# Stick-breaking attention with queries on partitions: reversed scans on VectorE for matrix sums on TensorE, and a gate product on GpSimd

## The chip, the cores and the metric

The kernel runs on one core of one Trainium2 chip. The number is the device time of one execution in microseconds (us), the median over repeated runs. Engines are named as in the profile: PE (TensorE matmul, with PEld for its weight loads), DVE (VectorE), ACT (ScalarE), POOL (GpSimd), SP (the queue that issues the weight transfers).

## What is computed

Two transformer blocks on 512 tokens of width 1024. The first has pooling, a gated unit, cross attention and a feed-forward part; the second has stick-breaking attention beside a gated 31-tap convolution, and a feed-forward part. The change is in the second block:

```python
def stick_breaking_attention(q, k, v):      # 8 heads of 64
    # A[t,s] = beta[t,s] * prod_{s<j<t} (1 - beta[t,j]),  beta = sigmoid(q_t.k_s / 8), s < t
    ...
        z = jnp.einsum("bqhd,bkhd->bhqk", qb, kb) * scale
        mask = s_idx < t_idx
        log_beta = jax.nn.log_sigmoid(z)
        log_one_minus = jnp.where(mask, jax.nn.log_sigmoid(-z), 0.0)
        tail = lax.cumsum(log_one_minus, axis=3, reverse=True) - log_one_minus
        weights = jnp.where(mask, jnp.exp(log_beta + tail), 0.0)
        outs.append(jnp.einsum("bhqk,bkhd->bqhd", weights, vb))
...
        c = glu_a * jax.nn.sigmoid(glu_b)
        c = causal_depthwise_conv(c, conv_dw_w[layer], conv_dw_b[layer])   # 31 taps
        c = jax.nn.silu(layer_norm(c, conv_ln_g[layer], conv_ln_b[layer]))
        mixed = jnp.concatenate([attn, c], axis=-1) @ w_out[layer]
```

## The kernel before

Every large product is made to nearly full fp32 precision from two rounded parts: three matmuls for each 128 x 128 piece of a weight (high x high, high x low, low x high, lines 1258 to 1260). The weights come as 216 blocks of 128 x 1024 through a ring of four slots. SP loads a block, ACT rounds it (`w_hi`, 1.05 us), POOL makes the rest (`w_lo`, two halves, L365), PE takes 24 matmuls of 512 columns with it. Each engine runs an order written out by hand, and semaphores join them.

The second block begins with the gated unit: 8 blocks `GLU` (gate and value in turns), then 4 blocks for the values `v2`, then 8 blocks for queries and keys (`qk_block(t)`, q and k of one pair of heads in turns). During `GLU` DVE multiplies the gate by the root of the norm (L1133), ACT takes the sigmoid (L646), DVE multiplies the value bank by the root (L1137) and then by the sigmoid (L1141). DVE fills the rest of its time with the 120 taps of the convolution (`conv_taps`, L1126); the first 68 stand before the q and k work, the other 52 are dealt out between its steps.

The attention goes by pairs of heads, each head's 1280 score columns in three PSUM banks, so two heads fill six banks. Keys are on the partitions and queries along the columns, in four tiles (512, 384, 256 and 128 columns, `TILES`). For a pair:

- `pair_scores(j)` on PE: eight matmuls, and six that add -1e30 where the key isn't before the query.
- `s_logs(hd)` on ACT: three activations over 1280 columns (a cap at 40, exp, and log of one plus that).
- `s_softplus(hd)` on DVE: the maximum with the scores (L1159), then three small adds into `later_sums` (L1165, L1168).
- `s_cumulate(hd)` on PE: nine fp32 matmuls with a matrix of -1 in a triangle (`neg_tri`) and one full of -1 (`neg_ones`), which add minus the sum over later keys to the scores in PSUM (L1582).
- `s_weights(hd)` on ACT: exp of that in two parts (L702). The next pair's scores take the same banks, so they wait for it (`s_att`).
- `pair_values(j)` on PE: weights times `v2`; ACT and DVE split the result in two parts (`pair_values_hi`, `pair_values_lo`).

Between them stand each q or k block's own steps: `qk_input` (DVE, frees the bank), `qk_squares_of` (ACT, which also rounds the next weight block), `qk_sum` (PE), `qk_rstd_of` (ACT, log and exp), `qk_apply` (DVE). After the last pair comes the layer norm of the convolution: POOL adds the four channel tiles (L443, wait for the last tap), PE sums over partitions (`ln_channel_sums(0)`), DVE subtracts the mean (`ln_centre`), ACT squares, POOL adds, PE sums again (`ln_channel_sums(1)`), ACT makes the root and, with another function table (L756), the silu. The output product `output2(m, ks)` can take the parts k = 0 to 3 (attention) early and needs k = 4 to 7 (convolution) at the end.

## Time and profile before

| | us |
|---|---|
| median of 3 runs | 1230.31 (1230.0 to 1230.79) |
| the profiled execution | 1230.45 |
| its span in the trace | 1228.7 |
| PE busy | 1222.5 (99%) |
| DVE busy | 593.9 (48%) |
| POOL busy | 585.3 (48%) |
| ACT busy | 505.4 (41%) |

The span is what the trace covers; 1.75 us of the execution lie around it. The granted TensorE clock is full in every slice. The stage of the change runs from 661 us (the gated unit) to about 843 us (the end of the first four output blocks' work). A busy PE is not PE at its peak: the record of a 512-column matmul is 0.39 us long, but one starts every 0.227 us.

### The profile page before, as it was taken

The numbers are of one execution on the slowest core, as the hardware profiler recorded it, in microseconds if no ns is written. First come the engines' busy times: TensorE is split into PE (matmuls) and PEld (weight loads), VectorE is DVE, ScalarE is ACT, GpSimd is POOL, SyncE is SP. The second block draws the span as 40 slices with busy tenths as digits, with TensorE's granted clock in tenths as the row PEclk, the third lists the DMA queues.
The fourth block names the chain that finished last, engine by engine and source line by source line (L and its number), as shares of the span: only waits on it lengthen the run. The fifth ranks groups of instructions, "written<-read, shape, count | busy, mean of one in ns | idle before, by whom it ended". The sixth has DMA issues, their size and how long they took to land.

```text
span 1228.7 us, 16447 instructions
## 1 busy us (share of the span) xinstructions
PE 1222.5 (99%) x5590; PEld 1004.1 (82%) x5590; DVE 593.9 (48%) x870; ACT 505.4 (41%) x677; POOL 585.3 (48%) x473
## 2 busy tenths in 40 slices
PE   9999999999999999999999999999999999999998
PEld 7988888888888888888888886768888888888887
DVE  6782435434653165414675898764333223321431
ACT  7532443343443144323464247675433223332331
POOL 5875553233445344463465652134444434444444
PEclk9999999999999999999999999999999999999999
DMA  7444332122232322232233221102222322223222
GB/s 299 138 138 135 105 103 69 52 69 69 103 102 103 103 85 87 101 120 72 77 125 103 103 86 52 35 18 86 87 102 88 117 86 102 93 83 116 81 77 82
DMA packets 34035, 118.41 MB, mean 96 GB/s; under 512 B 4033, under 2 KB 4161, under 8 KB 33857
## 3 DMA queue, kind: packets, MB, share of 16 engines
q1 hardware_dynamic: 33696, 117.49, 27.9%
q8 instruction: 34, 0.56, 0.2%
q10 hardware_dynamic: 288, 0.24, 0.1%
q14 instruction: 17, 0.13, 0.0%
HBM read 115.61 MB, written 2.10 MB: 96 GB/s over the span
## 4 chain that ended last, share of the span: by engine, by line
PE 93%; DVE 5%; ACT 1%; POOL 0%; issue 0%; POOLq 0%
PE ps L1258 29%; PE ps L1259 29%; PE ps L1260 29%; DVE ps L1126 2%; DVE slab L1126 2%; PE ps L1582 2%; PE ps L1425 1%; PE ps L1563 1%; PE ps L1324 0%; PE ps L1350 0%; PE ps L1623 0%; POOL squares L443 0%; PE ps L1440 0%; PE ps L1399 0%; PE ps L1536 0%
## 5 line engine op out<-in xcount | busy, mean ns | idle before, releaser
L365 POOL TENSOR_TENSOR w_lo<-w_raw,w_hi 128x512 fp32r<-128x512 f32 x430 | 557.3, 1320 | 610.3 <-ACT w_hi L476 355.8
L1258 PE MATMUL ps<-xg_hi,w_hi 128*128 128x512 f32 x960 | 375.8, 391 | 0.0
L1260 PE MATMUL ps<-xg_hi,w_lo 128*128 128x512 f32 x960 | 373.6, 389 | 0.0
L1259 PE MATMUL ps<-xg_lo,w_hi 128*128 128x512 f32 x960 | 373.6, 389 | 0.0
L1258 PE MATMUL ps<-y_hi,w_hi 128*128 128x512 f32 (+1 forms) x608 | 230.9, 380 | 0.0
L1259 PE MATMUL ps<-y_lo,w_hi 128*128 128x512 f32 (+1 forms) x608 | 229.8, 378 | 0.0
L1260 PE MATMUL ps<-y_hi,w_lo 128*128 128x512 f32 (+1 forms) x608 | 229.8, 378 | 0.0
L1260 PEld LDWEIGHTS ps<-xg_hi,w_lo 128*128 128x128 f32 x960 | 180.2, 188 | 37.7
L1258 PEld LDWEIGHTS ps<-xg_hi,w_hi 128*128 128x128 f32 x960 | 180.2, 188 | 37.7 <-issue 0.8
L1259 PEld LDWEIGHTS ps<-xg_lo,w_hi 128*128 128x128 f32 x960 | 180.2, 188 | 37.3 <-issue 0.5
L476 ACT ACTIVATE w_hi<-w_raw 128x1024 fp32r<-128x1024 f32 x124 | 130.4, 1051 | 126.1 <-PE ps L1260 126.1
L774 DVE TENSOR_TENSOR ps<-ps,rstd_bc 128x512 f32<-128x512 f32 x92 | 64.0, 698 | 184.7 <-PE ps L1260 182.6
L464 ACT ACTIVATE w_hi<-w_raw 128x1024 fp32r<-128x1024 f32 x91 | 96.0, 1055 | 96.2 <-PE ps L1260 79.9
L1259 PEld LDWEIGHTS ps<-y_lo,w_hi 128*128 128x128 f32 x608 | 114.4, 188 | 21.8 <-issue 0.5
L1258 PEld LDWEIGHTS ps<-y_hi,w_hi 128*128 128x128 f32 x608 | 114.4, 188 | 21.8 <-issue 0.6
L1260 PEld LDWEIGHTS ps<-y_hi,w_lo 128*128 128x128 f32 x608 | 114.4, 188 | 21.3
L517 ACT ACTIVATE slab<-ps,cols 128x512 f32<-128x512 f32 x66 | 51.3, 779 | 129.9 <-DVE ps L774 129.9
L892 DVE TENSOR_TENSOR h<-ps,h 128x512 f32<-128x512 f32 x32 | 22.1, 692 | 129.2 <-PE ps L1260 129.2
L523 ACT ACTIVATE slab<-slab 128x512 f32<-128x512 f32 x44 | 27.8, 632 | 120.2 <-DVE slab L872 120.2
L805 DVE TENSOR_TENSOR y_lo<-slab,y_hi 128x512 f32 (+1 forms) x52 | 37.9, 734 | 40.6 <-ACT y_hi L525 38.3
L525 ACT ACTIVATE y_hi<-slab 128x512 f32 x44 | 27.8, 632 | 66.1 <-DVE slab L878 44.9
L866 DVE SCALAR_TENSOR_TENSOR slab<-ps,cols,slab 128x511 f32<-128x511 f32 x66 | 49.0, 744 | 10.6 <-ACT slab L517 10.6
(218 smaller groups left out, 1064.1 us busy)
## 6 DMA issues: line engine op xcount, KB each, us to landing
w_raw<-weights SPq DMA_DIRECT2D x199, 512.0 KB, 3.2
w_raw<-weights SPq DMA_DIRECT2D x16, 384.0 KB, 2.9
out_t<-h SPq DMA_DIRECT2D x8, 256.0 KB, 2.0
h<-x_t SPq DMA_DIRECT2D x3, 512.0 KB, 8.3
slab<-mem_t SPq DMA_DIRECT2D x2, 512.0 KB, 10.6
slab<-mats_in SPq DMA_DIRECT2D x1, 1024.0 KB, 5.5
w_raw<-weights SPq DMA_DIRECT2D x2, 256.0 KB, 3.5
h<-x_t SPq DMA_DIRECT2D x2, 256.0 KB, 4.3
```

The lines of the kernel that those rows point to most:

```text
L365: nc.gpsimd.tensor_tensor(w_lo[:, s, half], w_raw[:, s, half], w_hi[:, s, half].bitcast(F32), ALU.subtract).then_inc(done, 1)
L464: nc.scalar.activation(w_hi[:, s, :], w_raw[:, s, :], ACT.Copy).then_inc(w_hi_ready, 1)
L476: nc.scalar.activation(w_hi[:, s, :], w_raw[:, s, :], ACT.Copy).then_inc(w_hi_ready, 1)
L517: nc.scalar.activation(acc[:, s + v, :], ps[:, s + v, :], ACT.Identity, scale=col(w, pair + (2 * n_w + v * FT)), bias=col(b, pair + v * FT ...
L523: nc.scalar.activation(acc[:, s, :], acc[:, s, :], ACT.Silu).then_inc(f_silu, 1)
L774: return nc.vector.tensor_tensor(out, ps[:, bank, 0:width], by[:, 0:width], ALU.mult)
L805: nc.vector.tensor_tensor(dst, src, hi.bitcast(F32), ALU.subtract).then_inc(y_lo_ready, 1)
L866: nc.vector.scalar_tensor_tensor(out=acc[:, s + v, 1:], in0=ps[:, s + v, 0:SEQ - 1], scalar=col(w, pair + (n_w + v * FT)), in1=acc[:, s + ...
L1126: nc.vector.scalar_tensor_tensor(out=conv_acc(i)[:, j:], in0=conv_in[:, i, 0:SEQ - j], scalar=col("conv_dw_w_2", (TAPS - 1 - j) * 4 + i), ...
L1258: pe.matmul(out, w[0], x[0], start=first, stop=False)
L1259: pe.matmul(out, w[0], x[1], start=False, stop=False)
L1260: return pe.matmul(out, w[1], x[0], start=False, stop=last)
```

## The change

**Layout.** The scores are made with queries on the partitions and keys along the columns: `pair_scores` takes q as the stationary and k as the moving operand. The tiles keep their sizes.

**Attention weights.** For each head ACT makes two sigmoids of the scores, beta into `took` and 1 - beta into the old stick tile, each over 1280 columns. DVE runs four `tensor_tensor_scan` over them with a reversed access pattern, state = (1 - beta) x state + beta, in place in `took` (`s_scan`, 512, 384, 256 and 128 columns). The result at key s is the sum of the weights of keys s and later. PE turns it with ten 128 x 128 transposes per head (`s_turn`) into the score banks, and ACT copies it out in one piece (`s_weights`, Copy over 1280 columns). The sum over later keys is not differenced again: the values are. `v2` becomes v[s] - v[s-1]: ACT issues two transfers that shift `v2` by a row, and POOL makes four subtractions (`v2_steps`).

**Function tables.** Sigmoid is not in the table set of log and exp, so ACT loads a table before each pair's sigmoids and another behind them: eight more table loads.

**Order.** `s_cumulate`, `s_logs`, `s_softplus` and `later_sums` are gone. `qk_block(5)` now stands ahead of `pair_values(0)`, `qk_block(6)` behind `pair_scores(2)`, and `s_turn(5)` behind `qk_block(7)`. `ln_channel_sums(0)` stood ahead of `output2(0, (2,))`; now it stands behind `pair_values(3)` and six output parts (m = 1 and 2, k = 0 to 2), and `ln_channel_sums(1)` behind four more. DVE leaves 4 taps behind the last scan.

**Gated unit.** POOL multiplies the sigmoid by the root (`glu_gate`), and DVE's product L1137 goes.

```diff
             for b in range(GLU, V2 + 4):
                 weights_lo_next(b)
+                if b < V2 and (b - GLU) % 2 == 0:
+                    i = (b - GLU) // 2
+                    pool.wait_ge(glu_sig, i + 1)
+                    nc.gpsimd.tensor_tensor(k2[:, i, :], k2[:, i, :], rstd_bc[:], ALU.mult).then_inc(glu_gate, 1)
...
-            for b in range(QK, WOUT2):
+            weights_lo_next(QK)
+            pool.wait_ge(v2_shifted, 32)
+            for t in range(ST):
+                nc.gpsimd.tensor_tensor(v2[:, t, :], v2[:, t, :], v2_before[:, t, :], ALU.subtract).then_inc(v2_steps, 1)
+                if t % 2:
+                    weights_lo_next(QK + 1 + t // 2)
+            for b in range(QK + 3, WOUT2):
                 if b == QK + 4:
-                    pool.wait_ge(s_later, 2)
+                    pool.wait_ge(s_summed, 2 * ST)
...
+            act.dma_start(v2_before[1:P, :, :], v2[0:P - 1, :, :]).then_inc(v2_shifted, 16)
+            act.dma_start(v2_before[0:1, 1:ST, :], v2[P - 1:P, 0:ST - 1, :]).then_inc(v2_shifted, 16)
...
+                nc.scalar.activation(took_of(hd), z_of(hd), ACT.Sigmoid).then_inc(s_parts, 1)
+                nc.scalar.activation(stick_of(hd), z_of(hd), ACT.Sigmoid, scale=-1.0).then_inc(s_parts, 1)
...
             def s_weights(hd):
-                for part, c in enumerate((FIRST, REST)):
-                    act.wait_ge(s_cum, 2 * hd + (2 if hd == SPLIT_HEAD else part + 1))
-                    nc.scalar.activation(stick_of(hd)[:, c], z_of(hd)[:, c], ACT.Exp).then_inc(s_att, 1)
+                act.wait_ge(s_turned, hd + 1)
+                nc.scalar.activation(stick_of(hd), z_of(hd), ACT.Copy).then_inc(s_att, 1)
...
+            def s_scan(hd):
+
+                dve.wait_ge(s_parts, 2 * hd + 2)
+                for bank, at, n in TILES:
+                    c = slice(bank * SEQ + at, bank * SEQ + at + n)
+                    took = backwards(took_of(hd)[:, c])
+                    nc.vector.tensor_tensor_scan(took, backwards(stick_of(hd)[:, c]), took, 0.0, ALU.mult,
+                                                 ALU.add).then_inc(s_summed, 1)
...
+            def s_turn(hd):
+
+                for n, t in enumerate((3, 2, 1, 0)):
+                    bank, at, _ = TILES[ST - 1 - t]
+                    pe.wait_ge(s_summed, ST * hd + n + 1)
+                    for key in range(t + 1):
+                        src = bank * SEQ + at + key * P
+                        to = AT[key] + (t - key) * P
+                        mm = pe.transpose(z_of(hd)[:, to:to + P], took_of(hd)[:, src:src + P], ident[:])
+                mm.then_inc(s_turned, 1)
```

PE, from the fourth root's sum to the second pair's scores: before, the sums over later keys of head 0 (the rows of head 1 read the same) and the start of pair 1.

```order
L1536 MATMUL ps<-squares,pair_ones 128x512 [waits qk_square]
L1582 MATMUL ps<-slab,neg_tri 128x512 [waits s_stick]
L1582 MATMUL ps<-slab,neg_ones 128x128
L1582 MATMUL ps<-later_sums,neg_ones 128x256 [waits s_later]
L1582 MATMUL ps<-slab,neg_tri 128x384
L1582 MATMUL ps<-slab,neg_tri 128x256
L1582 MATMUL ps<-slab,neg_tri 128x128
L1582 MATMUL ps<-slab,neg_ones 128x128 x2
L1582 MATMUL ps<-later_sums,neg_ones 128x128 [waits s_later]
```

The same place with the change: each tile's transposes wait for that tile's scan.

```order
L1539 MATMUL ps<-squares,pair_ones 128x512 [waits qk_square]
L1585 MATMUL ps<-ident,took 128x128 [waits s_summed]
L1585 MATMUL ps<-ident,took 128x128 x3
L1585 MATMUL ps<-ident,took 128x128 [waits s_summed]
L1585 MATMUL ps<-ident,took 128x128 x2
L1585 MATMUL ps<-ident,took 128x128 [waits s_summed]
L1585 MATMUL ps<-ident,took 128x128
L1585 MATMUL ps<-ident,took 128x128 [waits s_summed] x2
```

Nine matrix products that waited for `s_stick` and `s_later` have become ten transposes that wait for four scans; the last row's second instruction opens head 1.

ACT, around the scores of the last pair (heads 6 and 7): before, the root of the last k block, the split head 6 and head 7.

```order
L702 ACTIVATE slab<-ps 128x768 [waits s_cum]
L672 ACTIVATE slab<-ps,z_max 128x768 [waits s_out,s_z]
L674 ACTIVATE slab<-slab,z_max 128x768 [waits s_min]
L676 ACTIVATE slab<-slab 128x768 [waits s_exp]
L672 ACTIVATE slab<-ps,z_max 128x512
L674 ACTIVATE slab<-slab,z_max 128x512 [waits s_min]
L676 ACTIVATE slab<-slab 128x512 [waits s_exp]
L706 ACTIVATE y_hi<-ps 128x512 [waits s_out]
L670 ACTIVATE squares<-squares 128x1280 [waits s_last_min,s_out,s_z]
L676 ACTIVATE squares<-squares 128x1280 [waits s_exp]
```

The same place with the change.

```order
L694 ACTIVATE ps<-ps 128x512 [waits qk_log]
L685 ACT_TABLE_LOAD
L681 ACTIVATE took<-ps 128x1280 [waits s_out,s_turned,s_z]
L682 ACTIVATE slab<-ps 128x1280
L681 ACTIVATE took<-ps 128x1280 [waits s_out,s_turned,s_z]
L682 ACTIVATE squares<-ps 128x1280
L685 ACT_TABLE_LOAD
L714 ACTIVATE y_hi<-ps 128x512 [waits s_out]
L710 ACTIVATE slab<-ps 128x1280 [waits s_turned]
L710 ACTIVATE squares<-ps 128x1280 [waits s_turned]
```

The high part of pair 2's values (`y_hi`, L706 before, L714 now) stood between heads 6 and 7; now it stands behind both heads' sigmoids and a table load, and in DVE's order its low part stands between the scans of heads 6 and 7.

## Rows read from the trace of the kernel before

**Rows 1.** The page: busy time, and the chain that ended last, by engine.

```profile
PE 1222.5 (99%) x5590; PEld 1004.1 (82%) x5590; DVE 593.9 (48%) x870; ACT 505.4 (41%) x677; POOL 585.3 (48%) x473
...
PE 93%; DVE 5%; ACT 1%; POOL 0%; issue 0%; POOLq 0%
```

**Rows 2.** Busy time by stretch, each from one pair's scores to the next.

```profile
core 0: us, PE busy (x) PEld busy (x) DVE busy (x) ACT busy (x) POOL busy (x), PEclk, DMA share, GB/s
740.30:759.00 18.70, 17.83 (x89) 12.65 (x88) 18.10 (x25) 15.65 (x18) 5.49 (x4) 1.00 0.17 56
759.00:784.30 25.30, 25.30 (x128) 18.08 (x129) 18.96 (x28) 16.46 (x20) 5.10 (x4) 1.00 0.18 63
784.30:803.30 19.00, 19.00 (x102) 13.34 (x102) 13.47 (x22) 14.27 (x16) 3.79 (x3) 1.00 0.08 28
803.30:822.50 19.20, 18.97 (x102) 11.86 (x102) 13.57 (x22) 13.43 (x19) 6.38 (x5) 1.00 0.01 2
```

**Rows 3.** The chain in order of time: start, length, engine and line.

```profile
299.30 0.44 PE ps L1333 x4
...
758.10 0.86 PE ps L1536 x2
758.97 2.36 PE ps L1563 x16
...
762.15 2.30 PE ps L1623 x16
764.46 0.43 PE ps L1258
...
775.58 0.86 PE ps L1536 x2
...
795.44 3.48 PE ps L1582 x18
```

**Rows 4.** Timeline of ACT.

```profile
719.38 1.28 ACT L659 ACT_TABLE_LOAD   x1
720.67 1.09 ACT L690 ACTIVATE slab<-ps 128x512 f32<-128x512 f32 x2
...
752.54 0.62 ACT L696 ACTIVATE squares<-slab 128x512 f32<-128x512 f32 x1
753.07 1.04 ACT L464 ACTIVATE w_hi<-w_raw 128x1024 fp32r<-128x1024 f32 x1
754.02 0.64 ACT L682 ACTIVATE ps<-ps,eps_one 128x512 f32<-128x512 f32 x1
754.69 0.58 ACT L685 ACTIVATE ps<-ps 128x512 f32<-128x512 f32 x1
...
811.39 1.26 ACT L670 ACTIVATE squares<-squares 128x1280 f32<-128x1280 f32 x1
```

**Rows 5.** Timeline of DVE: start, length, operation, [idle before].

```profile
747.81 1.47 DVE L1159 TENSOR_TENSOR slab<-ps,slab 128x1280 f32<-128x1280 f32 x1
749.32 2.25 DVE L1165 TENSOR_TENSOR later_sums<-slab 128x128 f32<-128x128 f32 x2
...
780.47 5.14 DVE L1126 SCALAR_TENSOR_TENSOR slab<-slab,cols 128x491 f32<-128x491 f32 x7
...
792.73 0.49 DVE L1165 TENSOR_TENSOR later_sums<-slab 128x128 f32<-128x128 f32 x2
793.26 0.29 DVE L1168 TENSOR_TENSOR later_sums<-slab,later_sums 128x128 f32<-128x128 f32 x1
793.47 0.68 DVE L805 TENSOR_TENSOR y_lo<-ps,y_hi 128x512 fp32r<-128x512 f32 x1
```

**Rows 6.** Timeline of POOL: a weight block's low half pair, and the last channel adds.

```profile
748.87 2.56 POOL L365 TENSOR_TENSOR w_lo<-w_raw,w_hi 128x512 fp32r<-128x512 f32 x2 [8.62 <-ACT w_hi L464]
...
819.76 2.68 POOL L443 TENSOR_TENSOR squares<-squares,slab 128x512 f32<-128x512 f32 x2
```

**Rows 7.** Timeline of PE and DVE at the layer norm's second sum.

```profile
822.49 1.12 PE L1632 MATMUL ps<-squares,neg_ones 128*128 128x512 f32 x2 [0.19 <-POOL squares L443]
...
827.75 0.69 DVE L805 TENSOR_TENSOR y_lo<-slab,y_hi 128x512 fp32r<-128x512 f32 x1 [0.31 <-ACT y_hi L762]
...
831.86 0.69 DVE L805 TENSOR_TENSOR y_lo<-slab,y_hi 128x512 fp32r<-128x512 f32 x1 [0.68 <-ACT y_hi L762]
```

**Rows 8.** Groups of PE's instructions by form: the first ten matmuls, and warm ones alike.

```profile
L1582 PE MATMUL ps<-slab,neg_ones 128*128 128x128 f32 x36 | 6.0, 275 | 0.0
...
L1350 PE MATMUL ps<-neg_ones 128*128 128x128 f32 x20 | 4.6, 429 | 1.8 <-POOL eps_q L386 1.8
```

More of the change, by code:

```diff
@@ L164, in build @@
         xg_lo = sb("xg_lo", [P, DT, SEQ], F32R)
+        with nc.sbuf_tensor("took", [P, 2, DT * SEQ], F32) as took:
+            pass
         y_hi = sb("y_hi", [P, DT, SEQ], F32R)
@@ L713, in _ @@
             qk_rstd_of(2)
-            s_logs(0)
+            table(SIGMOIDS)
+            s_parts_of(0)
             qk_squares_of(3)
-            s_logs(1)
+            s_parts_of(1)
+            table(LOGS)
             qk_squares_of(4)
@@ L722, in _ @@
             qk_rstd_of(4)
-            s_logs(2)
-            pair_values_hi(0)
-            s_logs(3)
+            table(SIGMOIDS)
+            s_parts_of(2)
+            s_parts_of(3)
+            table(LOGS)
             qk_squares_of(5)
-            qk_squares_of(6)
             qk_rstd_of(5)
@@ L731, in _ @@
             s_weights(3)
+            table(SIGMOIDS)
+            pair_values_hi(0)
+            s_parts_of(4)
+            s_parts_of(5)
+            table(LOGS)
+            qk_squares_of(6)
+            pair_values_hi(1)
             qk_rstd_of(6)
-            s_logs(4)
-            pair_values_hi(1)
-            s_logs(5)
+            s_weights(4)
             qk_squares_of(7)
-            s_weights(4)
+            s_weights(5)
             qk_rstd_of(7)
-            s_weights(5)
-            s_logs(6)
+            table(SIGMOIDS)
+            s_parts_of(6)
+            s_parts_of(7)
+            table(LOGS)
             pair_values_hi(2)
-            s_logs(7)
             s_weights(6)
+            s_weights(7)
+            pair_values_hi(3)
             for i in range(4):
@@ L1202, in _ @@
             qk_apply(2)
-            conv_taps(7)
-            s_softplus(0)
+            conv_taps(6)
+            s_scan(0)
+            s_scan(1)
             qk_input(4)
-            s_softplus(1)
+            conv_taps(2)
             qk_apply(3)
-            conv_taps(4)
-            qk_apply(4)
-            conv_taps(5)
-            s_softplus(2)
-            pair_values_lo(0)
-            qk_input(5)
-            s_softplus(3)
-            conv_taps(2)
-            qk_input(6)
-            qk_apply(5)
-            conv_taps(7)
-            qk_apply(6)
-            conv_taps(4)
-            s_softplus(4)
-            pair_values_lo(1)
-            qk_input(7)
-            s_softplus(5)
-            qk_apply(7)
-            conv_taps(9)
-            dve.wait_ge(s_z, LAST_HEAD + 1)
-            dve.wait_ge(s_out, (LAST_HEAD - 4) // 2 + 1)
-            nc.vector.tensor_scalar(stick_of(LAST_HEAD), z_of(LAST_HEAD), Z_MAX, None, ALU.min).then_inc(s_last_min, 1)
-            s_softplus(6)
+            conv_taps(3)
+            qk_apply(4)
+            conv_taps(6)
+            s_scan(2)
+            qk_input(5)
+            s_scan(3)
+            conv_taps(2)
+            qk_apply(5)
+            pair_values_lo(0)
+            conv_taps(6)
+            s_scan(4)
+            qk_input(6)
+            s_scan(5)
+            pair_values_lo(1)
+            conv_taps(4)
+            qk_apply(6)
+            qk_input(7)
+            conv_taps(2)
+            qk_apply(7)
+            conv_taps(3)
+            s_scan(6)
             pair_values_lo(2)
-            s_softplus(7)
-            ln_centre()
+            s_scan(7)
+            conv_taps(len(tap_order))
             assert not tap_order
             pair_values_lo(3)
+            ln_centre()
             ln_apply()
@@ L1556, in pair_scores @@
                     pe.wait_ge(rounded, 2)
-                for tile in (0, 1, 3, 2):
-                    bank, at, n = TILES[tile]
-                    if j >= 1 and tile < 2:
-                        pe.wait_ge(s_att, 2 * (2 * j - 1) + tile + 1)
+                if j >= 1:
+                    pe.wait_ge(s_att, 2 * j)
+                for t in (3, 2, 0, 1):
+                    bank, at, n = TILES[ST - 1 - t]
                     for hd in heads:
                         r = slice(HD * (hd % 2), HD * (hd % 2) + HD)
-                        pe.matmul(ps[:, 3 * (hd % 2) + bank, at:at + n], k2[r, j, tile * P:(tile + 1) * P],
-                                  q2[r, j, tile * P:], start=tile != 3, stop=False, skip_group_check=True)
+                        pe.matmul(ps[:, 3 * (hd % 2) + bank, at:at + n], q2[r, j, t * P:(t + 1) * P],
+                                  k2[r, j, 0:n], start=t != 0, stop=False, skip_group_check=True)
@@ L1565, in pair_scores @@
                 for hd in heads:
                     bank = 3 * (hd % 2)
[L1567 to L1568 removed]
+                    pe.matmul(ps[:, bank, 3 * P:], ident_r[:], far_below_r[:], start=False, stop=False, skip_group_check=True)
+                    pe.matmul(ps[:, bank + 1, 2 * P:].rearrange("p (a t) -> p a t", t=P), ident_r[:],
@@ L1612, in pair_values @@
             def pair_values(j):
+                if j == 0:
+                    pe.wait_ge(v2_steps, ST)
                 if j < 2:
```

171 lines of the change are left out of this document (54 added, 117 removed).

## The prediction

> **What bounds the kernel now.** I read the page first: PE is busy for 99% of the span, and 93% of the chain that ended last is PE's [rows 1]. So the first reading is that every matmul taken away is time won. I then read the stage of the change pair by pair: PE is busy for all of it but 1 us, DVE for 18.1 of 18.7 us, 19.0 of 25.3, 13.5 of 19.0 and 13.6 of 19.2, ACT for 15.7, 16.5, 14.3 and 13.4 [rows 2]. The reader is to see that PE is full here only because its order holds work enough to cover a long round trip: scores on PE, three activations on ACT, the maximum and the small sums on DVE, the sums on PE, the exponential on ACT, and only then the next pair's scores, which take the same banks. Take PE's work out, and the round trip is what remains. Last comes the layer norm's row of waits at the end, for which the kernel keeps output parts back.
>
> **What the change takes from PE.** One head's sum over later keys costs 3.48 us [rows 3]; eight heads, 27.8 us. A transpose of 128 columns costs 0.11 us (four take 0.44) [rows 3], so ten per head 1.1 us, eight heads 8.8 us. PE's work falls by 19.0 us. Scores (3.2 us a pair, 758.97 to 762.15), values (2.30), a root's sum (0.86) and a block (764.46 to 775.58 for two, 5.5 each, 5.44 without the changeover) stay [rows 3].
>
> **What ACT does.** Its activation without a bias pointer over 1280 columns lasts 1.26 us [rows 4], and the next overlaps it by 0.1. Two sigmoids are 2.4 us where three activations stood, and the copy out is 1.2. A table load is 1.28 us, and ACT's next record stands right behind it [rows 4]. Eight more are 10.2 us; six of them lie in waits for PE or DVE, two stand on the path (before the high part of pair 0's values, and in the tail).
>
> The Trainium skill (ScalarE: Activation LUTs, What ACT_TABLE_LOAD costs) adds 1.38 us of drain to each load's 1.28. Rows 4 show the load alone, with no gap ahead of it or behind. By the page the two loads on the path would cost 2.8 us more, and the sum would be 1241.
>
> **What DVE does.** The maximum is 1.4 us apart from the next, three small sums add 0.75 [rows 5]: 2.2 us a head, 17 us in all, and 2.4 us of products in the gated unit go. The scan has no row. From below: one elementwise pass, 1280 columns and three more starts, 1.65 us a head. From above, by the nearest rows: it does a multiply and an add on each element and hands the result on, so two passes, 2.97 us (1.14, 0.88, 0.61 and 0.34 for the four tiles). I take two passes, since the add can't start before the multiply's result is there. A third pass (4.3 us) bounds it further out.
>
> The Trainium skill (DVE: opcode table, instruction layouts, handler registers and perf-mode slots, Datapath and trigger behaviour) says that the built-in scan runs at half throughput. No row here shows it; by the page the sum would be what I take.
>
> **The round trip laid out.** I start where before's scores(0) start, 740.3, and give each engine the durations above in its new order. The same laying out for the kernel before gives its last pair's scores 0.5 us and the norm's second sum 1.0 us late, so I trust it to about 1 us.
> - *Pair 0 to 1.* z of head 0 is there at 743.1. ACT has its parts at 745.6; DVE is in its taps until 747.5. Two scans end at 753.5, `qk_input(4)` at 754.1. Behind it in ACT's order: square, w_hi and root of t = 3 (0.5, 0.95 and 1.2, from 0.62, 1.04, 0.64 and 0.58 less overlaps) [rows 4], two copies (2.4): 759.3. PE stood at its wait from 753.8 but for one sum of 0.86. Before, scores(1) began at 758.97. All 4.8 us saved on PE are waited away, and 0.3 more.
> - *Pair 1 to 2.* Scores, block 5, values, root's sum: 771.1; root 1.2 and two copies 2.4: 774.9. PE's transposes (2.2) end before that; it waits 1.6. Before, 784.3 [rows 2], with another block in it.
> - *Pair 2 to 3.* Scores, block 6 (moved here), values, sum, turn(4): 788.0. Block 7 waits for pair 1's low part behind scan(5): 1.0. Then turn(5), 0.5 for the square, the sum: 796.9. Copy, root and `qk_apply(7)`: 800.0. Before, 803.2. In three pairs 14.4 us less work bring 3.2 us.
> - *The tail.* z of head 6 at 803.0, its parts at 805.4, scan(6) to 808.4. DVE's low part of pair 2 waits for ACT: head 7's sigmoids, a table load, the high part, 809.6. Scan(7) from 810.2 to 813.2, its last transposes 813.5, copy 814.9, values 817.2. Six output parts of 0.68 stand ahead of the first channel sum (the last four taps and POOL's adds end at 818.4): 821.3 to 822.2. Centring and squares, then three adds on POOL at 1.27 [rows 6]: 828.3. Before, this second sum began at 822.5 [rows 7]. PE meanwhile has four output parts, and waits 3.4 us.
> - *Behind it.* The convolution's low parts come 5.9 us (first) and 10.1 us (fourth) after that sum [rows 7]: 834.2 and 838.4. Before, PE had parts enough to reach 832.3 and took the sixteen last ones in 10.9 us, to 843.2. Now the first block's end waits for the fourth part, 839.1, and twelve parts follow: 847.2. All behind it is PE-bound as before. **+4.0 us.**
>
> **What POOL adds.** Two small sums took 2.25 us at 749.3, while POOL's pair of halves ran from 748.87 to 751.43, and 0.49 us at 792.7 without it [rows 5, 6]: +1.76. A DVE operation that reads two SBUF tiles waits for POOL. Seven taps begun at 780.47, as such a pair ended, took 5.14 us, some 0.6 too long [rows 5]. A pair thus costs DVE 0.6 to 1.8 us, 1.3 in the middle. The subtractions of `v2` are two pairs' worth more, all beside taps ahead of the first scan: up to 2.6, less 0.7 that the gated unit wins. The scans read two SBUF tiles too (the maximum read PSUM and did not wait), and the pairs of blocks 3, 5 and 6 fall on scans 0, 3 and 5: 3.5. That is 0 to 6; I take 4. Execution: 1230.45 + 4.0 + 4 = 1238.4, and against the median 1230.3, **1238.3 us**.
>
> **The rivals.**
> - *PE's work decides* (faster). If waits were short, 19.0 us go: 1211. For it: 99% [rows 1]. Against: rows 2 show DVE as full as PE in the first pair. One copy of a head and the root chain alone put scores(1) where it was.
> - *A scan as cheap as one pass, POOL hardly in the way* (no change). The same laying out with 1.65 us: scores(3) at 797.5, the second sum at 824.5, the end at 843.3, so +0.1 and up to 2.5 with POOL: 1230.3 to 1233. It decides below about 2 us a head.
> - *The clock* (slower than my forecast). The first twenty records of PE after its long wait last 429 ns where warm ones last 275 [rows 8], and start 0.23 instead of 0.11 us apart: 1.2 for 2.4 GHz. Granted clock reads 1.00 there, so only durations show it. Around scores(1), scores(3) and values(3) PE has 8 us with some 3 us of work. If the clock falls there, scores and values at half speed add 3.2 + 3.2 + 2.3, with blocks behind: +4 to +9, about 1244. It decides if waits of 3.5 us suffice, and before has none such behind its start.
>   The Trainium skill (TensorE: Matmul & The Clock Gate, Part 1) says an idle engine is put back to the lower clock.
> - *DVE saturates.* If POOL and DVE take turns instruction by instruction, each tap beside POOL waits 1.3, the first scan starts 6 us later, and the sum is +12.5: 1243. With a scan of three passes, 4.3 us a head, +13.5: 1244, and with POOL 1250.
>
> **How the numbers follow.** Forecast, +5 to +11: 0.48. Clock 0.18, saturation or slow scan 0.17: all slower. Cheap scan 0.11: within 0.2%, 2.5 us, which is about what a measurement tells from no change. PE decides, or some of the 19 us is kept: 0.06. Range: no less than the cheap scan without POOL, 1230; up to clock or saturation with the forecast's waits, 1248. Faster 0.06, same 0.11, slower 0.83.
>
> **What would show it.** Scan rows: 1.1 to 1.2 us for 512 columns and about 3 a head. PE idle ahead of pair_scores(1) 3 to 4 us, released by ACT's copy; ahead of pair_scores(3) by `qk_apply`. The second channel sum at 830 to 834. PE's busy time down by less than 19, since it waits. Taps beside the `v2` subtractions longer. Matmul records of 512 columns at 0.4 us throughout: if many last about twice that behind waits, the clock did it. Wrong would be: the second sum before 823, or scans far from 3 us a head.

## The result, and the profile after

The changed kernel takes **1271.53 us** (median of 4 runs, 1271.0 to 1272.28) against 1230.41 (4 runs, 1230.0 to 1230.79) beside it on the same chip: a ratio of **1.0335, 95% interval 1.0317 to 1.0353**, 41 us slower. The forecast was 1238.3, the range ended at 1248: the direction was right, and the size was not.

The page of the changed kernel: its span, busy time, granted clock, the queue that carried the two new transfers, and the chain that ended last.

```profile
span 1269.3 us, 16308 instructions
...
PE 1219.5 (96%) x5526; PEld 996.2 (78%) x5526; DVE 598.2 (47%) x864; ACT 502.5 (40%) x667; POOL 597.0 (47%) x479
...
PEclk9999999999999999999999976998999999999999
...
q10 hardware_dynamic: 448, 1.28, 0.3%
...
PE 90%; DVE 3%; ACT 3%; ACTq 2%; issue 1%; POOL 1%; DMA 0%; SPq 0%; POOLq 0%; DVEq 0%
```

Beside [rows 1], PE's share fell from 99% to 96%, and `ACTq` is new in the chain: ACT's instruction queue, issuing a transfer. The same stretches as in [rows 2], from each pair's scores to the next and to the norm's second sum (columns as there; the first one begins at 740.30, where the scores of pair 0 began before the change).

```profile
740.30:759.00 18.70, 15.96 (x53) 11.86 (x54) 8.13 (x13) 8.93 (x13) 2.51 (x2) 0.76 0.15 53
759.00:788.50 29.50, 16.56 (x72) 10.24 (x71) 20.53 (x22) 15.13 (x17) 17.85 (x12) 0.74 0.17 59
788.50:807.40 18.90, 17.01 (x86) 11.39 (x86) 16.04 (x21) 13.74 (x15) 2.91 (x2) 0.87 0.14 48
807.40:833.80 26.40, 21.20 (x112) 14.81 (x112) 19.52 (x27) 16.63 (x19) 5.95 (x5) 1.00 0.07 27
833.80:864.00 30.20, 24.39 (x115) 15.06 (x115) 14.67 (x21) 12.30 (x14) 7.03 (x6) 0.94 0.05 18
```

A leg is the way from one pair's scores to the next, or from the last scores to the norm's second sum. The last three legs take 18.9, 26.4 and 30.2 us where they were laid out with 15.6, 25.1 and 28.3, together 6.5 us more. The larger loss is ahead of them. Scores(0) stand 19.4 us late, and from there to scores(1) it is 28.8 us for 19.0.

The timeline of ACT tells the first half (start, length, operation, idle before it and what ended that).

```profile
719.65 1.23 ACTq L668 DMA_DIRECT2D slab<-slab  x1
720.91 19.15 ACTq L669 DMA_DIRECT2D slab<-slab  x1
740.09 1.28 ACT L670 ACT_TABLE_LOAD   x1 [20.48 <-issue]
...
775.31 1.24 ACT L681 ACTIVATE took<-ps 128x1280 f32<-128x1280 f32 x1 [8.84 <-POOL slab L437]
```

The first issue sends `v2`, shifted by one partition over 127 partitions, 1016 KB; the second, 6 KB on one partition, took 19.15 us to issue. The squares that ACT makes for the q and k blocks stood behind it, and PE and DVE behind those:

```profile
743.04 2.08 PE L1539 MATMUL ps<-squares,pair_ones 128*128 128x512 f32 x2 [15.96 <-ACT squares L705]
...
780.02 1.11 PE L1585 MATMUL ps<-ident,took 128*128 128x128 f32 x4 [7.92 <-DVE took L1171]
...
788.50 4.64 PE L1566 MATMUL ps<-slab 64*128 64x512 f32 x16 [2.40 <-ACT slab L710]
```

The first of these rows shows the clock too: PE had waited 15.96 us, the granted clock stood at 0.50 (1.2 GHz) from 734 to 749, and the sum of two matmuls took 2.08 us where it takes 1.02 at 752.41. A part of the 19.4 us is the clock's.

The second half is in POOL's timeline. Its subtractions waited for the landing until 765.66, 46 us after the issue. Head 1's sigmoids (the first of them above, 775.31) wait for the last subtraction, because the output of the second one overlies `v2_before`.

```profile
765.66 4.17 POOL L437 TENSOR_TENSOR slab<-slab 128x512 f32<-128x512 f32 x2 [19.07 <-DMA slab<-slab]
769.79 2.98 POOL L362 TENSOR_TENSOR w_lo<-w_raw,w_hi 128x512 fp32r<-128x512 f32 x2
772.74 2.48 POOL L437 TENSOR_TENSOR slab<-slab 128x512 f32<-128x512 f32 x2
```

Why so slow? These windows show the DMA share and GB/s last, with the granted clock ahead of them.

```profile
724.00:734.00 10.00, 3.09 (x14) 2.23 (x12) 5.03 (x12) 0.00 (x0) 0.00 (x0) 0.90 0.06 25
734.00:744.00 10.00, 0.96 (x1) 0.50 (x2) 0.00 (x0) 3.90 (x6) 0.00 (x0) 0.50 0.06 27
```

0.06 is one engine of sixteen, at 25 to 27 GB/s; 1016 KB at that rate are 39 to 42 us, most of the 46. The Trainium skill (DMA: Bandwidth & Descriptors, "Why a DMA increments its semaphore by 16 and not by 1") states that a transfer is spread over the largest number of engines up to 16 that divides its slowest dimension, and that 127 partitions put everything on one. The trace agrees with it: 0.06.

### The profile page after: what moved, and what is told of

It is laid out like the page before. It is cut to its first block, busy times and chain, and to the rows that moved or that the text cites. A ratio compares the mean times of both kernels' runs of the same rounds, so it can differ in the third digit from the quotient of the medians.

```text
span 1269.3 us, 16308 instructions
## 1 busy us (share of the span) xinstructions
PE 1219.5 (96%) x5526; PEld 996.2 (78%) x5526; DVE 598.2 (47%) x864; ACT 502.5 (40%) x667; POOL 597.0 (47%) x479
## 3 DMA queue, kind: packets, MB, share of 16 engines
q10 hardware_dynamic: 448, 1.28, 0.3%
## 4 chain that ended last, share of the span: by engine, by line
PE 90%; DVE 3%; ACT 3%; ACTq 2%; issue 1%; POOL 1%; DMA 0%; SPq 0%; POOLq 0%; DVEq 0%
PE ps L1261 28%; PE ps L1263 28%; PE ps L1262 28%; DVE took L1171 2%; ACTq L669 2%; PE ps L1428 1%; PE ps L1566 1%; PE ps L1318 1%; PE ps L1317 1%; PE ps L1319 1%; DMA h<-x_t 0%; PE ps L1327 0%; POOL slab L437 0%; DVE y_lo L822 0%; DVE slab L1143 0%
## 5 line engine op out<-in xcount | busy, mean ns | idle before, releaser
L791 DVE TENSOR_TENSOR ps<-ps,rstd_bc 128x512 f32<-128x512 f32 x88 | 61.2, 698 | 180.3 <-PE ps L1263 178.5
L883 DVE SCALAR_TENSOR_TENSOR slab<-ps,cols,slab 128x511 f32<-128x511 f32 x66 | 49.0, 744 | 10.6 <-ACT slab L524 10.6
```

The lines of the kernel that those rows point to most:

```text
L791: return nc.vector.tensor_tensor(out, ps[:, bank, 0:width], by[:, 0:width], ALU.mult)
L883: nc.vector.scalar_tensor_tensor(out=acc[:, s + v, 1:], in0=ps[:, s + v, 0:SEQ - 1], scalar=col(w, pair + (n_w + v * FT)), in1=acc[:, s + ...
```

## The experiments

All ratios are against the kernel before, run beside each.

**Cut the transfer.**

```diff
-            act.dma_start(v2_before[1:P, :, :], v2[0:P - 1, :, :]).then_inc(v2_shifted, 16)
+            act.dma_start(v2_before[1:113, :, :], v2[0:112, :, :]).then_inc(v2_shifted, 16)
+            act.dma_start(v2_before[113:P, :, :], v2[112:P - 1, :, :]).then_inc(v2_shifted, 16)
...
-            pool.wait_ge(v2_shifted, 32)
+            pool.wait_ge(v2_shifted, 48)
```

> The changed kernel, with the transfer over 127 partitions cut into one over 112 and one over 15; the one-partition transfer stays third, all on ACT's queue. In the trace of the changed kernel the 1016 KB moved at 23 to 28 GB/s with a DMA share of 0.06 to 0.07, one engine's worth of 16, landed about 45 us after the issue, and ACT's second issue took 19.15 us. Theory A (a transfer over 127 partitions runs on one engine, and this is what the time went to; the Trainium skill, DMA: Bandwidth & Descriptors, Why a DMA increments its semaphore by 16 and not by 1, states that 127 partitions put everything on one engine): the transfers land within 6 us of the first issue, no issue takes over 3 us, scores(0) ends near 741 us, and the time is 1236 to 1246 us, near the 1238 that was forecast before any trace of the change. Rival B (SBUF to SBUF transfers are slow whatever their shape, a few of ACT's queue): landing stays 30 us or later and the time is 1260 to 1272. Rival C (the loss is the clock or POOL and DVE in each other's way, and the transfer only delayed what would have waited anyway): transfers land early and the time is still above 1255.

1249.95 us (1247.67 to 1250.28), ratio 1.0155 (1.0138 to 1.0172): 21.6 of the 41 us go with one transfer cut in two. The issues and their landing (KB, median us from issue to landing), and the window in which they fall, with the DMA share and GB/s last:

```profile
slab<-slab ACTq DMA_DIRECT2D x1, 896.0 KB, 6.1
...
slab<-slab ACTq DMA_DIRECT2D x1, 120.0 KB, 7.2
...
719.00:724.00 5.00, 5.00 (x23) 4.14 (x23) 5.00 (x11) 0.89 (x1) 0.97 (x1) 1.00 0.75 184
```

ACT issues the three in 0.62, 1.38 and 2.00 us, and scores(0) begin at 741.60. The DMA share is 0.75 in this window, for 0.32 in the same window of the changed kernel. It is theory A in kind. Two of its numbers were missed: the time is 4 us above its range, and the last of the three (6 KB, issued at 721.08) landed about 9 us after the first issue, not within 6. Rival B is out: a transfer from SBUF to SBUF is not slow as such. Rival C is out too, at 1250 for over 1255.

**The same transfers in the other order.**

```diff
-            act.dma_start(v2_before[1:P, :, :], v2[0:P - 1, :, :]).then_inc(v2_shifted, 16)
             act.dma_start(v2_before[0:1, 1:ST, :], v2[P - 1:P, 0:ST - 1, :]).then_inc(v2_shifted, 16)
+            act.dma_start(v2_before[1:P, :, :], v2[0:P - 1, :, :]).then_inc(v2_shifted, 16)
```

> The changed kernel with the two transfers in the other order on ACT's queue: the one-partition one first, that over 127 partitions second. It parts two costs of the slow transfer: ACT held for 19 us by the issue behind it, and its late landing. Theory A1 (ACT is held because the second issue stands behind a transfer that one DMA engine works off, but the late landing alone would have cost as much): neither issue takes over 3 us, the first squares and scores(0) come at 740 to 743 instead of 759.7, yet the shift still lands near 765 us, head 1's sigmoid still starts at 774 to 776, and the time is 1260 to 1272. Theory A2 (the hold of ACT is its own 19 us): the time falls by 12 to 20, to 1252 to 1260. Rival (the issue of the long transfer itself can hold ACT, whichever comes second): the second issue takes over 15 us again and nothing changes.

1271.64 us (1270.8 to 1272.06), ratio 1.0339 (1.0321 to 1.0356). Timeline of ACT in this kernel:

```profile
719.12 0.64 ACTq L668 DMA_DIRECT2D slab<-slab  x1
719.79 1.16 ACTq L669 DMA_DIRECT2D slab<-slab  x1
720.98 1.28 ACT L670 ACT_TABLE_LOAD   x1 [1.89 <-issue]
...
772.71 1.24 ACT L681 ACTIVATE took<-ps 128x1280 f32<-128x1280 f32 x1 [25.92 <-POOL slab L437]
```

ACT is free, scores(0) begin at 740.00 and not at 759.68, and not a microsecond is won: head 1's sigmoid still waits, and nearly all of the 19 us move from the wait ahead of scores(0) to the one behind them. Head 1's sigmoid comes 2.6 us earlier (772.71), a little ahead of the 774 to 776 expected, and so do scores(1). That is gone by scores(3), with scores(2) taking 4.05 us for 2.43. That is A1. ACT was held by an issue *behind* the long transfer, and the late landing alone costs the same 22 us. The largest wait in a trace isn't what its removal is worth.

**Without the transfers, and without the subtractions too.**

```diff
-            pool.wait_ge(v2_shifted, 32)
+            pool.wait_ge(v2_ready, ST)
...
-                nc.gpsimd.tensor_tensor(v2[:, t, :], v2[:, t, :], v2_before[:, t, :], ALU.subtract).then_inc(v2_steps, 1)
+                nc.gpsimd.tensor_tensor(v2[:, t, :], v2[:, t, :], rstd_bc[:], ALU.subtract).then_inc(v2_steps, 1)
...
-            act.wait_ge(v2_first, 1)
-            act.dma_start(v2_before[1:P, :, :], v2[0:P - 1, :, :]).then_inc(v2_shifted, 16)
-            act.dma_start(v2_before[0:1, 1:ST, :], v2[P - 1:P, 0:ST - 1, :]).then_inc(v2_shifted, 16)
```

> The changed kernel without the two transfers: POOL subtracts the root's broadcast row from each of v2's four tiles in place of the shifted v2 (same shapes, same engine, same place), so the values used in the attention are others and the output is not the reference's. It leaves every cost of the change but the transfers. Theory A: 1235 to 1245 us, within 3 us of the kernel whose transfer is cut in two; PE waits before scores(1), (2), (3) are 3 to 5 us. If POOL against DVE, the clock or the table loads were the cause, it stays above 1255.

1245.35 us (1245.24 to 1245.53), ratio 1.0124 (1.0107 to 1.0141).

> As the kernel without transfers, and without POOL's four subtractions too (v2 is used as it is, the output is not the reference's). POOL loses 4 x 2.0 to 2.9 us between 721 and 745. Theory: the subtractions lie under PE's blocks and the first scores, so the time is within 1.5 us of the kernel without transfers. Rival (they push POOL's low halves of the QK blocks late, and PE's blocks with them): 3 to 6 us faster than the kernel without transfers.

This one leaves out the `tensor_tensor` line of the diff above and the waits for `v2_steps`. 1242.87 us (1242.49 to 1244.11), ratio 1.0106 (1.0089 to 1.0123): 2.5 us less, between the two expectations.

So the shift costs 4.6 us even when cut, and the subtractions 2.5. The issues are little of the 4.6: with them ACT loads its table 4.0 us later (723.12 for 719.12), but scores(0), (1) and (2) begin only 0.7 to 1.1 us later. Scores(3) begin 4.3 us later, and ahead of them PE ran slowly: behind the same wait of 1.59 us scores(2) took 4.12 us for 2.43, and the granted clock in 780 to 785 and 785 to 790 was 0.80 and 0.86 where it was 1.00 without transfers. Why the clock fell in one and not in the other isn't shown.

What my working spoke of, everything but the transfers, costs 15 us where I forecast 8. Four experiments look for the other 7, all on the kernel with the cut transfer (1249.95). Each has four runs that lie 1.8 to 4.4 us apart, so a gain of 3.5 us is known to about 2. In the kernel without transfers three things stand out on PE and DVE:

```profile
762.81 4.64 PE L1563 MATMUL ps<-slab 64*128 64x512 f32 x16 [2.40 <-ACT slab L707]
...
781.65 2.43 PE L1563 MATMUL ps<-slab 64*128 64x512 f32 x16 [1.59 <-DVE slab L1159]
...
808.03 3.96 PE L1563 MATMUL ps<-slab 64*128 64x512 f32 x16 [2.89 <-DVE slab L1159]
```

```profile
745.19 5.02 DVE L1140 SCALAR_TENSOR_TENSOR slab<-slab,cols 128x500 f32<-128x500 f32 x6
750.13 6.92 DVE L1168 TENSOR_TENSOR_SCAN took<-slab,took 128x512 f32<-128x512 f32 x8
...
774.64 5.03 DVE L1168 TENSOR_TENSOR_SCAN took<-squares,took 128x512 f32<-128x512 f32 x4
```

Scores last 4.64 and 3.96 us behind waits of 2.40 and 2.89 us, and 2.43 behind one of 1.59 (the clock). Six taps hold the first scan to 750.13, though ACT had its inputs by 746.2 (DVE's order). A head's scan lasts 5.03 beside a pair of operations on POOL.

**Taps off the path of the first scan.**

```diff
             qk_apply(2)
-            conv_taps(6)
+            conv_taps(1)
...
             qk_apply(7)
-            conv_taps(3)
+            conv_taps(8)
```

> The changed kernel with the cut transfer (1249.95 us), and on DVE five of the six convolution taps that stand ahead of the first head's scan put behind the last QK tile's gain instead, where DVE waited 4.5 us in the kernel without transfers (scan 6 idle 4.48 before it at 815.0). In the kernel without transfers the first scan began at 750.13, though the second sigmoid of its head had ended at 746.2: DVE had 5.02 us of taps to do, four us of them after that. Theory D (DVE's order of work holds the round trip of pair 0; PE's wait before scores(1) is for the copy behind that scan): scores(1) comes 3 to 4 us earlier and the time is 1245.5 to 1248. Rival (what comes early is waited for elsewhere, scores(1) also needs the QK tile 3 by ACT's root, which ended at 760.4): scores(1) comes at most 1.5 us earlier, the time moves by under 1 us.

1246.43 us (1243.33 to 1247.7), ratio 1.0125 (1.0108 to 1.0142): 3.5 less. Scores(1) begin at 760.94 and not at 763.51, 2.6 us earlier, and scores(2) and (3) keep that. Theory D, half a microsecond short of its 3 to 4 at that place.

**Work that nobody reads in PE's waits.**

```diff
+            def fill(n, bank):
+                for _ in range(n):
+                    pe.matmul(ps[:, bank, 2 * P:].rearrange("p (a t) -> p a t", t=P), ident_r[:],
+                              far_below_r[:].rearrange("p (a t) -> p a t", a=1).broadcast_to([P, 2, P]), start=True, stop=True,
+                              skip_group_check=True)
...
             qk_sum(4)
+            pe.wait_ge(qk_ready, 4)
+            fill(12, 7)

             pair_scores(1)
```

> The changed kernel with the cut transfer (1249.95 us), with 62 matmuls that nobody reads (128x128 by 256 columns, f32r, about 0.11 us each at full clock) put into PE's waits: 18 around the turns of heads 0 and 1, 12 before scores(1), 16 before the last QK block and 16 before scores(3). The result doesn't depend on them. In the trace without transfers the granted clock was 0.76 in 755 to 760, 0.50 in 760 to 765, 0.72 in 765 to 770, 0.88 and 0.78 in 805 to 815; scores(1) took 4.64 us against 2.43 at full clock, scores(3) 3.96, the two sums of QK tile 4 2.07 against 1.02. Theory C (the clock falls because PE is little busy in these stretches, and costs 2.2 + 1.5 + 1.0 us here): with them the granted clock stays 1.00 there, scores(1) and scores(3) take 2.4 to 2.5 us each, and the time falls by 2 to 5 us to 1245 to 1248. Rival C2 (the fall of the clock lies beside waits and the extra work delays as much as it brings, or the clock doesn't follow PE's work): the time is within 1 us of 1250 or up to 2 us slower.

These are 12 of the 62; the others stand in the same way around the turns of heads 0 and 1, before the last QK block and before scores(3). 1243.65 us (1243.29 to 1245.05), ratio 1.011 (1.0093 to 1.0127): 6.3 less, above the 2 to 5 expected. Three windows of the kernel with the cut transfer,

```profile
755.00:760.00 5.00, 3.07 (x13) 1.64 (x13) 4.61 (x7) 1.64 (x3) 0.00 (x0) 0.91 0.00 0
760.00:765.00 5.00, 2.60 (x6) 0.91 (x6) 3.71 (x5) 4.92 (x7) 2.49 (x2) 0.50 0.24 66
765.00:770.00 5.00, 5.00 (x23) 3.38 (x20) 4.18 (x7) 1.82 (x2) 0.00 (x0) 0.57 0.11 42
```

and the last two with the added matmuls: the granted clock is 1.00 in both, and scores(1) last 2.43 us.

```profile
760.00:765.00 5.00, 3.24 (x19) 2.18 (x20) 3.48 (x5) 4.92 (x8) 2.50 (x2) 1.00 0.20 54
765.00:770.00 5.00, 5.00 (x32) 3.89 (x29) 5.00 (x8) 4.33 (x4) 0.00 (x0) 1.00 0.15 54
```

The clock rival of the prediction was real: a granted 0.50, the level of 1.2 GHz, behind a stretch in which PE was 3.07 of 5 us busy. Scores(1) begin no earlier (763.80 for 763.51); the gain comes behind them, 2.5 us by scores(2) and 4.0 by scores(3). Not every place was mended: scores(2) still took 4.06 us here.

**The tail in another order.** The first channel sum ahead of the last pair's values, the taps done before scan 6, DVE's centring and ACT's squares ahead of that pair's parts.

```diff
             s_turn(7)
+            pe.wait_ge(y_lo_ready, Y_MIX2 + 3)
+            ln_channel_sums(0)
             pe.wait_ge(s_att, 7)
...
             s_scan(7)
-            conv_taps(len(tap_order))
-            assert not tap_order
+            ln_centre()
             pair_values_lo(3)
-            ln_centre()
```

> The changed kernel with the cut transfer (1249.95 us) and another order around the last pair: five taps from ahead of the first scan and the four behind the last scan go to DVE's waits ahead of scan 6 (all taps done there), the first channel sum stands on PE ahead of the last pair's values, DVE centres ahead of that pair's low part, and ACT squares ahead of its high part. Without transfers the tail was: last scan ended 822.8, four taps to 825.3, POOL's total 828.0, first channel sum and centring 832.0 to 834.5, POOL's second total 838.2, roots at 839.5; before the change that second sum came at 822.5, 19.3 us behind scores(3), and without transfers 31.4 behind it. Theory E (the tail's added 12 us come from the taps, totals and sums lined up behind the last scan): the second channel sum comes 23 to 26 us behind scores(3) and the time falls by 6 to 10 us, to 1240 to 1244. Rival (PE has blocks of output to do in that wait, so that the sum isn't what it waits for): falls by under 3 us.

The other lines of the edit take the first sum from where it stood and move taps and squares. 1241.3 us (1240.1 to 1242.93), ratio 1.0086 (1.0069 to 1.0103): 8.7 less, of which the taps alone were 3.5. The second sum came 25.7 us behind scores(3), for 29.9. (Without transfers it is 30.3; the 31.4 of the expectation is too much.) In this kernel it began at 836.68 with no wait, in PE's order behind output blocks, though POOL had its inputs by 833.3, and DVE waited 7.66 us for what follows it: its place was the limit.

**POOL's low halves kept off the scans of heads 3 and 5.**

```diff
                 if b == QK + 4:
-                    pool.wait_ge(s_summed, 2 * ST)
+                    pool.wait_ge(s_summed, 4 * ST)
+                if b == QK + 5:
+                    pool.wait_ge(s_summed, 6 * ST)
```

> The changed kernel with the cut transfer (1249.95 us), POOL's low halves of two weight blocks held back until heads 3 and 5 are scanned (it waits for more scans before them), so that they no longer fall beside scans: those of heads 3 and 5 took 5.03 and 5.01 us with a pair beside them against 2.97 alone. Theory P (each meeting costs DVE 2.05 us and PE waits for it, as before scores(2), where it waited 1.6 us for DVE's gain): both scans take 3.0 us and the time falls by 1 to 4 us, to 1246 to 1249. Rival P2 (the low halves are needed, PE waits for the later blocks, or the pair falls beside the next DVE work and costs as much there): within 1 us of 1250, or slower.

1246.2 us (1244.66 to 1247.23), ratio 1.0125 (1.0108 to 1.0142): 3.8 less, and both scans take 2.96 us. Head 3's scan and scores(2) in this kernel, then scores(2) in the kernel with the cut transfer:

```profile
776.04 2.96 DVE L1174 TENSOR_TENSOR_SCAN took<-squares,took 128x512 f32<-128x512 f32 x4
...
782.48 2.43 PE L1569 MATMUL ps<-slab 64*128 64x512 f32 x16 [1.55 <-ACT squares L713]
```

```profile
782.71 4.12 PE L1567 MATMUL ps<-slab 64*128 64x512 f32 x16 [1.59 <-DVE slab L1163]
```

That a meeting costs DVE 2 us is shown. That PE waited for it is not, for head 3: its scan is 2.07 us shorter, and scores(2) begin 0.2 us earlier, since ACT's copy is now what comes last. Then they take 2.43 us for 4.12, and scores(3) begin 4.3 us earlier. The clock is in the 3.8 with the scans, and the two aren't parted.

**One part of the change on the kernel before: the gated unit's sigmoid times the root on POOL.**

```diff
+                if b < V2 and (b - GLU) % 2 == 0:
+                    i = (b - GLU) // 2
+                    pool.wait_ge(glu_sig, i + 1)
+                    nc.gpsimd.tensor_tensor(k2[:, i, :], k2[:, i, :], rstd_bc[:], ALU.mult).then_inc(glu_gate, 1)
...
-                multiply_by_rstd(ps[:, bank, :], GLU + 2 * i + 1, bank).then_inc(vstep, 1)
```

> The kernel before with one part of the change alone: the gated unit's sigmoid is multiplied by the root on POOL (4 x about 1.3 us) and the product with the PSUM tile is made from that, DVE losing four 0.69 us operations and an own wait between them. PE was 70.00 of 70.00 us busy between 650 and 720 in the kernel before. Theory: no change, 1229.5 to 1231.5 us, since nothing there is waited for by PE; DVE's taps come 3 us earlier at best and it waits for them nowhere. Rival (POOL's later low halves stop PE, or DVE is held by the gate): 1232 to 1235. Rival (DVE's spare time brings QK's inputs and scores(0) forward, and with them PE's one wait of 0.87 us): 1228.5 to 1229.5.

1230.23 us (1229.76 to 1230.5, 11 runs), ratio 0.9998 (0.9989 to 1.0007). This part is free and brings nothing.

**Everything together.** The parts above in one kernel; besides, `v2_before` in the first four tiles of `y_hi`, the subtractions behind the first two scans, and the second channel sum ahead of the fourth output block.

> The changed kernel with everything that took time off it, in one: the transfer cut in three; v2's shifted copy in y_hi's first four tiles, so that head 1's sigmoid needn't wait for the subtractions, which POOL does behind the scans of heads 0 and 1; POOL's low halves held back until heads 3 and 5 are scanned; taps taken from ahead of the first scan and behind the last one and put where DVE waits; the first channel sum ahead of the last pair's values and the second ahead of the fourth output block; and the matmuls that nobody reads in PE's waits. Against the kernel with the cut transfer (1249.95 us) the parts alone gave 3.5 to 3.8 (taps; low halves apart), 6.3 (matmuls in the waits) and 8.7 (tail, in which the taps are). Theory (the parts lie in different legs and add, but those before scores(1) overlap, the taps' gain being in the tail's): 1231 to 1236 us, still no faster than the kernel before, because three to four waits of 1.5 to 3 us for copies and gains of the scan's way stay. Rival (what the change saves PE, 19 us of work, comes out once PE waits little): 1222 to 1229, faster than before. Rival 2 (the gains are the same few us, each): 1238 to 1242.

1232.85 us (1231.84 to 1234.46, 11 runs), ratio 1.0020 (1.0011 to 1.0029). The time lies in the theory's range, and its two rivals are out. 8.7, 6.3 and 3.8 us add to 18.8, and 17.1 were won against the 1249.95. That doesn't show that the parts add: the place of `v2_before` and of the second sum are in it and weren't run alone, and the next run takes one part out without a loss. The trace shows the added matmuls still standing in the way of scores(1), so two more:

> The kernel with all parts together (1232.85 us), without the 62 matmuls that nobody reads. Alone, on the kernel with the cut transfer, they gave 6.3 us. Theory C (they hold the clock up in the waits of the round trip, and the waits are still there): 2 to 6 us slower than with them, 1235 to 1239, with a granted clock of 0.5 to 0.8 somewhere in 755 to 765 and beside scores(3). Rival (with the waits mostly gone they are only load: 12 of them began at 758.1 and ended at 760.9, after the copies that scores(1) waits for had ended at 759.4): 1230 to 1232.5, faster than with them.

1232.77 us (1231.98 to 1233.7), ratio 1.0020 (1.0011 to 1.0029): level with the kernel that has them. Theory C's time fell here, and the rival's range was missed by 0.3. The clock does fall (granted 0.82 in 750 to 760, 0.66 in 800 to 810, where it was 0.92 and 1.00), but what the added matmuls gave alone they don't give here. Without them scores(1) run slowly but begin sooner, and scores(2) stand at the same place, 777.07 for 777.15. First without, then with them:

```profile
759.24 4.38 PE L1563 MATMUL ps<-slab 64*128 64x512 f32 x16 [3.35 <-ACT slab L709]
777.07 2.43 PE L1563 MATMUL ps<-slab 64*128 64x512 f32 x16 [1.55 <-ACT squares L709]
```

```profile
760.86 2.84 PE L1563 MATMUL ps<-slab 64*128 64x512 f32 x16
777.15 2.43 PE L1563 MATMUL ps<-slab 64*128 64x512 f32 x16 [1.55 <-ACT squares L709]
```

> The kernel with all parts together (1232.85 us), trimmed by its trace: 5 instead of 12 of the unread matmuls before scores(1), 8 instead of 16 before the last QK block, 10 instead of 16 before scores(3) (they ended 1.5, 0 and 0.3 us after what PE waited for); one of the taps between the input of QK tile 4 and the gain of tile 3 behind it, since PE waited 1.92 us for that gain; and the first channel sum ahead of head 7's turn, where PE waited for scans while the sum's inputs were there. Theory (each of these stood in the round trip): 1.5 to 4 us faster, 1229 to 1231.5, level with the kernel before. Rival (fewer matmuls in the waits let the clock fall again): 1233 to 1237.

1232.89 us (1231.33 to 1233.49), ratio 1.0019 (1.0010 to 1.0028). The trims brought scores(3) forward by 1.4 us (801.94) and the second sum by 0.9 (825.72), and the median not at all; that expectation fell. In the profiled execution the span was 1230.2 for 1231.1.

No version beat the kernel before. In the last one the way from scores(0) to the second sum is 19.0, 17.2, 25.3 and 23.8 us: 85.3, against 82.2 before the change, where the four are 18.6, 25.3, 19.0 and 19.3. The two in the middle each hold other blocks than before, and are together 1.8 us shorter; the loss is in the last one, 4.5 us. There head 6's scan met POOL's adds for the channel sum and took 5.01 us from 808.22. Two windows further up, in the same kernel:

```profile
760.00:770.00 10.00, 10.00 (x50) 6.79 (x48) 10.00 (x16) 7.66 (x7) 0.00 (x0) 0.92 0.01 2
...
780.00:790.00 10.00, 10.00 (x55) 7.01 (x54) 10.00 (x16) 8.81 (x10) 0.90 (x1) 1.00 0.01 2
```

DVE is busy for all of both, but so is PE, so they don't tell which of them sets the pace. My reading, not shown, is that the way through the scans has become the limit, in the last leg above all. A version with fewer taps beside the scans, or with POOL's adds off head 6's, wasn't tried.

## Why the prediction was wrong

- **PE's work** fell as counted (144 matmul records gone, 80 transposes come: 5590 to 5526) and none of it became time. PE busy went from 1222.5 to 1219.5, not down by 19. Slow matmuls are a part of the difference: the scores' records grew from 9.8 to 13.4 us in all, those of the roots' sums from 8.2 to 10.6. The rest I can't place. That the round trip is what remains when PE's work is taken out was right.
- **The step that failed: the shift of `v2`.** The working named "the subtractions of `v2`" and never priced the two transfers that feed them, neither their issue on ACT's queue nor their landing. Every instruction of a moved or added step counts, its DMAs too. Cut in two it is worth 4.6 us, as written 26 (1271.5 less 1245.4). The trace of before gave no warning: its load of 1024 KB landed in 5.5 us, and priced by that the shift would have stood in the sum with some 6 us. What sets it apart is its 127 partitions; every transfer of the kernel before takes all 128 of its tile. So the transfers belonged in the range as a term without a row.
- **Scores(0) at 740.3** failed with it (759.68). Without the transfers it is 740.87.
- **The scan** was sized right: 2.97 us a head (two passes: 2.97), in heads 2, 4, 6 and 7. The other four met POOL: 5.0 us in heads 1, 3 and 5, and 6.06 in head 0. The cheap and the slow scan are both out. Timeline of DVE, head 2, then head 3 with a pair of POOL's low halves beside it, then head 4:

```profile
796.27 2.97 DVE L1171 TENSOR_TENSOR_SCAN took<-slab,took 128x512 f32<-128x512 f32 x4 [2.10 <-ACT slab L682]
...
800.35 5.03 DVE L1171 TENSOR_TENSOR_SCAN took<-squares,took 128x512 f32<-128x512 f32 x4
...
813.42 2.96 DVE L1171 TENSOR_TENSOR_SCAN took<-slab,took 128x512 f32<-128x512 f32 x4
```

- **POOL in the way** was right in kind and too small: a pair costs a scan 2.05 us, not 1.3, and it was 4 us in my sum. Keeping two pairs away gave 3.8 us (the clock is in that), leaving the subtractions out 2.5.
- **DVE ahead of the first scan**: I had it in its taps until 747.5, it was 750.13 without transfers, the taps being held up by POOL too (the last six took 5.02 us, six others without POOL 3.95). Moving five of them gave 3.5 us. The rival in which DVE saturates had that scan 6 us later, and it was 2.6.
- **The clock** stood as a rival at 0.18, with +4 to +9 on top of the forecast. It came: 6.3 us go with the added matmuls in the kernel with the cut transfer. PE waited only 2.40 us ahead of scores(1), where the rival asked for 3.5 and my sign for 3 to 4, and the clock fell all the same. The forecast had such waits in it and should have had their clock in it too. That the rival's "about 1244" is near the 1245.35 without transfers is in part luck, since POOL's larger size is in that as well.
- **The table loads** last 1.28 us. The 1.38 us of drain that the Trainium skill (ScalarE: Activation LUTs, What ACT_TABLE_LOAD costs) adds isn't seen: in the kernel with the cut transfer the root ends at 741.95, the load stands at 741.97, and again there is no gap.
- **The tail** was laid out with a second sum 28.3 us behind scores(3): 30.3 in the changed kernel, and PE's wait there 3.51 for my 3.4. The sum came at 864.0 (838.3 without transfers), where I had 828.3 and a sign of 830 to 834.

Together: the forecast of +8 is +15 without the transfers, +20 with them cut, +41 as written. The +15 is inside the stated range, so the transfers are what carried the time out of it. How the 7 us between 8 and 15 divide among clock, POOL and taps isn't shown: what each gave alone (6.3, 3.8 and 3.5) overlaps, and was measured with the transfer in.

## What to carry to other kernels

Price a transfer like any other instruction: how many partitions it covers, which queue issues it, and what stands behind both; one over 127 partitions took 46 us where 112 and 15 took 6 to 7. Where a forecast contains waits on PE, it contains their clock too, and where a change moves work to DVE, count the POOL pairs that meet it. A wait that vanishes shows its worth only once the next one is known: 19 us came off ACT here and the time stayed the same. And where an experiment moves PE's waits, compare the length of the same matmuls before calling the gain that of the edit: scores(2) took 2.43 us in some of these kernels and over 4 in others.

## What the runs showed of the hardware

- Issuing a 6 KB transfer behind a 1016 KB one on the same queue held ACT for 19.15 us. In the other order the two issues took 0.64 and 1.16 us.
- A transfer within SBUF over 127 partitions moved 25 to 27 GB/s at a DMA share of 0.06; 1016 KB landed 46 us after the issue. Over 112 partitions 896 KB landed in 6.1 us, over 15 partitions 120 KB in 7.2 us.
- A multiply-add scan over 1280 columns in four pieces, read and written backwards, took 2.97 us, and 5.0 with a pair of POOL's 128x512 subtractions (the low halves of a weight block) beside it.
- A pair's scores took 2.43 us at a granted clock of 1.00 and 4.64 us at 0.50.
- 62 added matmuls made one kernel 6.3 us faster and another no faster: the clock they keep is worth what PE's speed is worth there.
